# Order of work in the openings of four blocked feed-forward networks: weight halves, input sums, sums of weights and the mean square

## What is computed

```python
def rmsnorm_2(x, gain):
    x32 = x.astype(jnp.float32)
    y = x32 * lax.rsqrt(jnp.mean(x32 * x32, axis=-1, keepdims=True) + EPS)
    return (y * gain.astype(jnp.float32)).astype(x.dtype)

def swiglu(h, w_gate, w_up, w_down):
    return (jax.nn.silu(h @ w_gate) * (h @ w_up)) @ w_down

    for i in range(DEPTH_2):                       # 2 layers
        h = rmsnorm_2(x, ffn1_norm[i])
        x = x + FFN_HALF * swiglu(h, ffn1_w_gate[i], ffn1_w_up[i], ffn1_w_down[i])
        ...                                        # mixer
        h = rmsnorm_2(x, ffn2_norm[i])
        x = x + FFN_HALF * swiglu(h, ffn2_w_gate[i], ffn2_w_up[i], ffn2_w_down[i])
```

## Time and profile before

| | |
|---|---|
| median of 3 runs | 2554.8 us (2551.88 to 2556.8) |
| the profiled execution's own time | 2551.45 us |
| its span | 2550.1 us |
| TensorE (PE) busy | 2472.7 us, 97% |
| VectorE (DVE) busy | 1794.0 us, 70% |
| ScalarE (ACT) busy | 1145.6 us, 45% |
| GpSimd (POOL) busy | 393.7 us, 15% |

### The profile page before, as it was taken

How to read it: one execution, slowest core, us unless ns; L and a number is a source line. 1 busy time by engine, 2 the same in 40 slices (tenths; PEclk the granted TensorE clock), 3 DMA queues, 4 the chain that set the end, 5 groups by cost and what they waited for, 6 DMA issues and landing times. The chain is left out here.

```text
span 2550.1 us, 36066 instructions
## 1 busy us (share of the span) xinstructions
PE 2472.7 (97%) x14234; PEld 2156.9 (85%) x14234; DVE 1794.0 (70%) x2879; ACT 1145.6 (45%) x1987; POOL 393.7 (15%) x301
## 2 busy tenths in 40 slices
PE   8999999999998999999899999999999999899999
PEld 7767777888886889898789897989998888699998
DVE  5896655565636868687768687868777566687776
ACT  4485443444323535355435354534354454453433
POOL 3673403222203000002000001000001431100000
PEclk9999999999999999999999999999999999999999
DMA  5211312333231333332233332323232112232323
GB/s 172 73 44 58 107 43 68 107 93 97 93 99 56 95 103 104 97 104 69 89 100 100 100 104 95 108 91 110 90 100 80 48 44 67 73 110 87 112 83 100
DMA packets 66520, 227.75 MB, mean 89 GB/s; under 512 B 7216, under 2 KB 8752, under 8 KB 66352
## 3 DMA queue, kind: packets, MB, share of 16 engines
q1 hardware_dynamic: 66352, 225.44, 28.4%
HBM read 223.31 MB, written 2.10 MB: 88 GB/s over the span
## 5 line engine op out<-in xcount | busy, mean ns | idle before, releaser
L526 DVE TENSOR_TENSOR wl<-raw,wh 128x1024 fp32r<-128x1024 f32 (+2 forms) x511 | 500.8, 984 | 246.6 <-ACT wh L517 244.3
L517 ACT ACTIVATE wh<-raw 128x1024 fp32r<-128x1024 f32 (+2 forms) x511 | 415.9, 835 | 482.5 <-PE main L581 244.9
L645 POOL TENSOR_TENSOR acc<-acc,sq 128x512 f32<-128x512 f32 (+1 forms) x88 | 125.4, 1425 | 1279.8 <-ACT sq L640 1274.5
L579 PE MATMUL main<-hxh,wh 128*128 128x512 f32 x624 | 251.6, 403 | 22.9 <-DVE wl L526 16.6
L580 PE MATMUL main<-hxl,wh 128*128 128x512 f32 x624 | 247.2, 396 | 0.0
L581 PE MATMUL main<-hxh,wl 128*128 128x512 f32 x624 | 246.7, 395 | 0.0
L526 DVE TENSOR_TENSOR wl<-sum,wh 128x512 fp32r<-128x512 f32 x288 | 195.0, 687 | 31.1 <-ACT wh L517 29.0
L517 ACT ACTIVATE wh<-sum 128x512 fp32r<-128x512 f32 x288 | 169.1, 623 | 101.5 <-PE main L581 49.8
L579 PEld LDWEIGHTS main<-hxh,wh 128*128 128x128 f32 x624 | 120.1, 192 | 53.1 <-issue 18.0
L1872 PE MATMUL score<-th,wh 128*128 128x256 f32 x504 | 143.5, 285 | 0.7 <-ACT kept L1979 0.4
L1873 PE MATMUL score<-tl,wh 128*128 128x256 f32 x504 | 142.6, 283 | 0.0
(11 more groups left out here) (519 smaller groups left out, 7067.3 us busy)
## 6 DMA issues: line engine op xcount, KB each, us to landing
raw<-in_wts SPq DMA_DIRECT2D x375, 512.0 KB, 3.5
raw<-in_wts SPq DMA_DIRECT2D x52, 384.0 KB, 3.0
x<-in_xT SPq DMA_DIRECT2D x4, 512.0 KB, 7.3
out<-x SPq DMA_DIRECT2D x8, 256.0 KB, 2.0
memx<-in_memT SPq DMA_DIRECT2D x1, 1024.0 KB, 9.6
raw<-in_wts SPq DMA_DIRECT2D x4, 256.0 KB, 2.6
band<-in_pool SPq DMA_DIRECT2D x1, 768.0 KB, 4.2
rope<-in_rope SPq DMA_DIRECT2D x1, 512.0 KB, 7.0
```

The lines of the kernel that those rows point to most:

```text
L517: e.activation(halves_of(wh, i), src, ACT.Copy).then_inc(*sig.up("weight_high", ("high", i)))
L526: e.tensor_tensor(halves_of(wl, i), src, f(halves_of(wh, i)), ALU.subtract) \
L579: e.matmul(o, ah, bh, start=start, stop=False)
L645: e.tensor_tensor(acc[:, 0:n], acc[:, 0:n], sq_turn(nm).of(("sq", nm, k))[:, 0:n], ALU.add) \
```

## The change

Nothing is added to the arithmetic and nothing is taken from it; instructions change places in the lists. In f10, f20 and f21 the sums of the input (`left_copy_scalar`, `turned_sums_vector` and their splits) move from step 0 behind the splits of weight tiles 3 and 4, to steps 2 to 4. In f11 (`EARLY`) they stay at step 0, but the last part of them moves ahead of weight tile 5. In all four networks the sums of weights of tile 3 move behind the mean square, to step 4, and the mean square stands at step 4 ahead of them. In f20, f11 and f21 TensorE's square sums move from behind product 2 to behind product 3, its spreading of the rows from behind product 3 to behind product 4, and `keep_rows` from step 4 to step 5, as f10 had it.

```diff
+        EARLY = ("f11",)
...
             elif which == GATE:
                 linear(e, u, g[:, :], normed(nm))
-                if c == 1 and nm not in LATE:
-                    square_sums(e, nm, KC - 1)
-                if c == 2 and nm in LATE:
+                if c == 2:
                     spread_rows(e, nm, ("root", nm))
             else:
                 linear(e, u + 1, p[:, :], normed(nm))
-                if c == 1 and nm in LATE:
+                if c == 1:
                     square_sums(e, nm, KC - 1)
-                elif c == 1:
-                    spread_rows(e, nm, ("root", nm))
...
-                    if rnd == 0 and s == 0:
+                    if rnd == 0 and s == (0 if nm in EARLY else 2):
                         for k in range(4):
                             left_copy_scalar(e, nm, k)
-                        for k in range(3):
+                        for k in range(3 if nm in EARLY else 1):
                             turned_high_scalar(e, nm, k)
+                    if rnd == 0 and nm not in EARLY and s == 3:
+                        for k in range(1, 3):
+                            turned_high_scalar(e, nm, k)
+                    if rnd == 0 and s == (2 if nm in EARLY else 3):
+                        turned_high_scalar(e, nm, 3)
                     if which:
                         weights_ahead(high, e, part_of(nm, c, which))
-                    if rnd == 0 and s == 2:
-                        turned_high_scalar(e, nm, 3)
-                    if rnd == 0 and s == (5 if nm in LATE else 4):
+                    if rnd == 0 and s == 5:
                         keep_rows(e, nm)
...
-                    if rnd == 0 and s == (4 if nm in LATE else 3):
+                    if rnd == 0 and s == (0 if nm in EARLY else 2):
+                        turned_sums_vector(e, nm, 0)
+                        turned_sums_vector(e, nm, 1)
+                        turned_low_vector(e, nm, 0)
+                    if rnd == 0 and s == (0 if nm in EARLY else 3):
+                        turned_sums_vector(e, nm, 2)
+                        turned_low_vector(e, nm, 1)
+                    if rnd == 0 and s == (2 if nm in EARLY else 3):
+                        turned_sums_vector(e, nm, 3)
+                        turned_low_vector(e, nm, 2)
+                    if rnd == 0 and s == 4:
                         mean_square(e, nm, 1.0 / D)
+                    if rnd == 0 and s == (2 if nm in EARLY else 4):
+                        turned_low_vector(e, nm, 3)
...
                     if which:
-                        weights_ahead(sum_weights, e, part_of(nm, c, which), AHEAD + 3)
+                        if rnd or s > 3:
+                            weights_ahead(sum_weights, e, part_of(nm, c, which), AHEAD + 3)
                         weights_ahead(low, e, part_of(nm, c, which))
-                    if rnd == 0 and s == 2:
-                        turned_sums_vector(e, nm, 3)
-                        turned_low_vector(e, nm, 2)
-                    if rnd == 0 and s == 3:
-                        turned_low_vector(e, nm, 3)
```

## The result

The changed kernel took 2522.3 us (median of 4 runs, 2521.13 to 2522.99) against 2554.2 for the kernel before beside it: ratio 0.9874, 95% interval 0.9857 to 0.9891, 31.9 us less. The forecast was 35 us less, 2519.8, with a range of 2510 to 2532. The span of the profiled execution went from 2550.1 to 2519.8 us.

What follows compares the result with a forecast made beforehand. The order of VectorE's list at the four openings was taken as the bound. Savings of 7.3 (f10), 10.5 (f20), 5.8 (f11) and 11.3 (f21) make 35 us: 2519.8 against the median 2554.8, range 2510 to 2532.

Steps and rivals of the forecast that it cites:

- The order of VectorE's list, not its speed: At the four openings, the order of VectorE's instructions makes TensorE wait: low halves 17.4 us, inverse root 17.2 us.
- f20, f21, f11: Openings of these networks: product 7 starts sooner, saving 10.5 us in f20, 11.3 in f21 and 5.8 in f11.
- the 1.5 to 2.5 that I had named as a sign: In f20, product 7 should wait 1.5 to 2.5 us for VectorE's gate multiplication.
- f10: f10's opening: product 7 at 847.6 instead of 854.93, saving 7.3 us, with a rows' wait of 3.9 us left.
- GpSimd adds squares until 823.8: In f10, VectorE instructions beside GpSimd's adds take 1.0 us more until then; low halves 3 and 4 take 2.1 each.
- The Trainium skill's rule: In f10, VectorE's two-SBUF-input instructions and GpSimd's exclude each other on shared ports; f10 would save 1.2 us less.
- The clock: Clock loss of 1.6 us behind f10's rows' wait; none charged for new waits at product 7, 1.6 each as other end.
- the clock eats a part: Rival: each wait left costs 1.6 us, VectorE's list 1 us longer per network; 25 us left, 2530; 14 in 100.
- Past product 7: Rounds behind the openings: every list in the old order, VectorE standing to TensorE as before, so costed at nothing.
- Slower, by the clock alone: Rival: short waits hold TensorE at 1.2 GHz through products 4 and 5, perhaps 6 and 7: 2561; 4 in 100.
- the rest goes too: Rival: ScalarE and VectorE leave no waits in the openings: 48 us gained, 2507; half of it 1 in 10.

Runs made afterwards that it cites:

- two others: The kernel with the change in f10 alone (2548.7 us) and the changed kernel run again (2523.0 us): f10's stretch 32.55 and 32.57 us.
- the repeated one: The changed kernel itself run and profiled again, nothing altered: 2523.0 us, ratio 0.9878 against the kernel before.
- the kernel with light adds: Changed kernel with GpSimd's adds of squares ahead of f10 covering only 4 of 512 columns (f10's mean square wrong for 508 tokens): 2514.1 us.
- the kernel with both edits: Changed kernel with rows kept ahead of high halves 10 and 11, and VectorE's mean square earlier in f10, f20, f21: 2516.5 us, again 2515.6.
- The kernel with f10's sums moved as well: Rows kept earlier, mean square earlier, plus f10's three sums of weights of tiles 3 and 4 behind the third gate multiplication: 2514.9 us.

## Why the prediction was right, and where it was off

- **The bound.** "The order of VectorE's list, not its speed": shown. The same instructions in another order gave 30.9 us in the stretches, and each half of the reordering took away its own wait.
- **f20, f21, f11.** Product 7 at 27.62, 27.09 and 26.12 us behind product 2 against 27.3, 27.0 and 25.75: gains of 10.2, 11.2 and 5.5 where the sum had 10.5, 11.3 and 5.8. The rows' wait in f20 was 1.27 for 0.7: I had costed the root at 1.78 from the mean square to the rows, and it took 2.31 (1221.97 to 1224.28), because a longer VectorE instruction stands behind the mean square now (below). It cost nothing at product 7, since VectorE's list was the later one, as forecast. The wait ahead of product 7 was 1.4 us in f20 and f21, a little under the 1.5 to 2.5 that I had named as a sign.
- **f10** is the term that was mis-sized: 4.0 us in the first profile and 5.3 in two others, for 7.3. The step "GpSimd adds squares until 823.8" failed. I took the end of the adds from the trace of before and counted how much of VectorE's list fits in front of it: two low halves and two input sums behind the low half of tile 2. In both traces it is the number that is the same: six instructions are drawn out by about 1.0 us each, before one low half and five input sums (814.70 to 824.05), in the changed kernel three low halves and three input sums, since the longer low halves put off the end of the adds (13.02 us instead of 11.38). So a third input sum was drawn out, to 1.41 us. Counted from product 2's start the mean square came at 20.6 instead of 19.3 us, the root took 0.5 longer, and the rows waited 5.42 instead of 3.9. Behind it product 5 lost more clock than the 1.6 that I charged: it took 8.0 instead of 5.44 us in this execution, 6.7 in the repeated one. The mechanism itself is shown by the kernel with light adds. The last drawn-out input sum on VectorE, before and then in the changed kernel:

```profile
822.56 1.49 DVE L1961 SCALAR_TENSOR_TENSOR tsum<-x,colsb,tsum 128x256 f32<-128x256 f32 x1
```

```profile
823.81 1.41 DVE L1964 TENSOR_TENSOR tsum<-tsum 128x256 f32<-128x256 f32 x1
```

- **The Trainium skill's rule** on the shared ports (SBUF — State Buffer, "SBUF: two separate sides"), which I had set at 1.2 us less for f10, pointed to the side on which the sum was off. This case agrees with it as far as it goes: VectorE's instructions were drawn out beside the adds, and the adds took 13.02 us instead of 11.38 beside the longer ones.
- **The clock.** In the changed kernel nothing was lost at the short waits: the products behind waits of 0.7 us (f10, granted clock 1.00 from 815 to 835) and of 1.3 to 1.5 us (f20, f11, f21) had their full length. But that I charged nothing at product 7 was luck in part. I had the waits there at 2.1 us, and they came out at 1.4. In the kernels in which the wait ahead of product 7 was 1.9 to 2.8 us, five of eight such waits were followed by the low clock, four at a price of 1.5 us and one of 2.6, and three were not (below). The rival "the clock eats a part" was therefore nearer than it looks from the result. Behind the one long wait of the changed kernel, f10's, the granted clock fell to 0.50, 1.2 GHz:

```profile
815.00:835.00 20.00, 18.43 (x84) 14.72 (x83) 19.72 (x23) 8.26 (x11) 9.22 (x6) 1.00 0.40 131
835.00:840.00 5.00, 0.50 (x3) 0.53 (x4) 4.46 (x8) 1.62 (x4) 1.94 (x1) 0.87 0.00 0
840.00:845.00 5.00, 5.00 (x14) 4.02 (x13) 4.07 (x7) 2.51 (x5) 0.00 (x0) 0.50 0.01 3
```

- **Past product 7** nothing was given back in the first round: 186.4 us from there to the first product by `w_down` before, 185.6 after. Over all that lies outside the stretches the profiles say 2404.5 and 2405.1 us, but they scatter too much to show it by themselves. That the rounds have little cover against a later list of VectorE was only seen when an experiment used it up.
- **Two sums of the rivals** were off, with no effect on the forecast. "The clock eats a part": five further waits at 1.6 and four times 1 us are 12, so 23 us would be left, not 25. "Slower, by the clock alone": products 6 and 7 at the low clock cost 1.1 us each (12 matmuls of 128x256 at 0.21 instead of 0.12 us apart, as measured in the kernel with both edits), 9 us for all eight, so it would be about 12 us lost and not 6.
- **The forecast's rival "the rest goes too"** didn't come, for the reason given against it; moving the mean square alone gave nothing, moving it with the kept rows 6.5 us more. The eight runs of that kernel (2514.6 to 2518.0) lie clear of the eight of the changed one (2518.8 to 2527.2). How much of it is the mean square's is open: keeping the rows earlier alone gave 3.3 us, and from product 2 to the first product by `w_down` the two kernels are 0.3 us apart. The kernel with f10's sums moved as well, at 2514.9, can't be told from it by time.

## What to carry to other kernels

When a fast engine waits for one with a written-out list, make a timetable of the slow engine's list up to the next instruction that frees something, and compare it with the fast engine's own work; the later of the two is the answer, and the fast engine's waits must not be added up. Put instructions that are wanted soon ahead of those that wait for transfers which these same instructions set going. And follow a list that is cut short at one point beyond that point: where the engine is nearly full afterwards, work pushed behind a deadline comes back as many short waits, and a clock loss can stand right behind the point that was measured.

## Not expected of the hardware

**The root on GpSimd grows with what VectorE does beside it.** It is one instruction on 4 columns. With VectorE idle it takes 1.02 us, and as much beside an instruction of 0.68 us that has one of its two inputs in PSUM (before, at 333.33). With an input sum of 0.48 us behind the mean square it took 1.20 (the kernel with both edits, f10), with a sum of weights of 0.68 us 1.40 (before, f20), with a `tl` of 1.22 us 1.94 (changed, f10): each time VectorE's instruction plus 0.72. The root alone (before, ahead of the openings), and then the first of the three, VectorE and GpSimd:

```profile
796.26 1.02 POOL L677 TENSOR_TENSOR stat<-stat,mhalf 128x4 f32<-128x4 f32 x1 [15.99 <-DVE stat L670]
```

```profile
833.12 0.48 DVE L1958 SCALAR_TENSOR_TENSOR tsum<-x,colsb,tsum 128x256 f32<-128x256 f32 x1
```

```profile
833.28 1.20 POOL L677 TENSOR_TENSOR stat<-stat,mhalf 128x4 f32<-128x4 f32 x1 [7.78 <-DVE stat L670]
```

**The same wait costs different amounts of clock.** Behind 5.4 us of wait in f10, product 5 took 8.0 us in one execution of the changed kernel and 6.7 in another. It is the whole of the difference between 33.90 and 32.57. Ahead of product 7 waits of 1.88 (f20), 2.00 (f10, twice) and 2.13 us (f21) were followed by a loss of 1.5 us each, one of 2.54 (f10) by 2.6 us (those in f10 stand a product behind another wait), and waits of 1.89 (f20, twice) and even 2.78 us (f20) by none. So the length of a wait alone does not tell here whether the clock falls behind it.

**Unchanged code scatters.** Outside the four stretches the profiled executions of kernels with the same lists took 2404 to 2411 us. The changed kernel in its first and its repeated profile, windows of 100 us (the granted clock is the third number from the right):

```profile
100.00:200.00 100.00, 92.21 (x501) 67.56 (x501) 93.57 (x161) 77.84 (x156) 75.23 (x57) 1.00 0.15 48
```

```profile
100.00:200.00 100.00, 94.03 (x490) 70.17 (x488) 92.78 (x159) 74.91 (x150) 73.81 (x56) 0.95 0.16 48
```

The same stretch of the program ran at a granted clock of 1.00 and of 0.95, and product 2 of f10 started at 816.58 and at 821.86. Why the clock fell there is open. For gains of a few us the stretch between two fixed instructions is a better measure than the whole time, if the second one stands far enough behind to take in a clock loss: the stretch to product 7 missed the ones that came behind it.
